# A two-block transformer kernel: token sums, head sums, gate scaling and turned blocks of the first mixer rearranged

## The reference

```python
h = rms_norm(x, g_mix_norm[l])
z = h @ w_in[l]
q_lat, kv_lat, k_rope = z[..., :o1], z[..., o1:o2], z[..., o2:o3]
uv, pin = z[..., o3:o4], z[..., o4:]
a = mla_mixer(q_lat, kv_lat, k_rope, ...)      # 4 heads: latents normed, up-projected, heads normed,
                                               # rope, causal softmax(q k / sqrt(96)) @ v -> 512 columns
gm = sgu_mixer(uv, g_v, w_spatial, b_spatial)  # below -> 256 columns
po = pool_mixer(pin, w_pool, pool_scale)       # running means over 2, 4, 8, 16 tokens, times w_pool -> 256
mix = concatenate([rms_norm(a, g_out_mla[l]), rms_norm(gm, g_out_sgu[l]), rms_norm(po, g_out_pool[l])])
x = x + mix @ w_out[l]
x = x + (silu(rms_norm(x) @ w_gate[l]) * (rms_norm(x) @ w_up[l])) @ w_down[l]

# sgu_mixer:
v = rms_norm(v, g_v)
w = w_spatial * tril(ones(128, 128))
z = einsum('hts,bcshd->bcthd', w, v_in_chunks_of_128) + b_spatial
return u * z
```

## Time and profile before

| | us |
|---|---|
| runs of the kernel | 3192.84, 3186.21, 3187.82 (median 3187.82) |
| the profiled execution, its own time | 3193.49 |
| its span in the profile | 3191.7 |
| mean granted TensorE clock | 0.986 |
| busy share of the span | PE 98%, PEld 79%, POOL 60%, DVE 47%, ACT 23% |
| chain that ended last, by engine | PE 89%, DVE 6%, issue 2%, ACT 2% |

### The profile page before, as it was taken

One profiled execution on the slowest core, in us unless ns is written; L12 is line 12 of the kernel. 1 busy time (PEld: TensorE's weight loads), 2 busy tenths in 40 slices (PEclk: granted clock), 3 DMA queues, 4 the chain that ended last, 5 costly groups with the idle time before them and its releaser, 6 DMA issues.

```text
span 3191.7 us, 41998 instructions
## 1 busy us (share of the span) xinstructions
PE 3132.2 (98%) x15408; PEld 2520.4 (79%) x15408; DVE 1498.8 (47%) x2570; ACT 739.4 (23%) x1525; POOL 1903.7 (60%) x885
## 2 busy tenths in 40 slices
PE   8999999999999999999999999999999999999998
PEld 7778888877888888876588888888787668888887
DVE  4664430356453042886545554214388653545411
ACT  4410100331010033434701101012343560111000
POOL 4277787427877877001088777787700118878775
PEclk9999999989999999999999999999999999999999
DMA  3133232103232222112032323332211103332332
GB/s 123 47 101 99 93 98 98 67 27 102 98 99 94 97 91 94 48 34 80 8 94 98 101 96 94 99 99 86 93 47 42 66 17 96 99 96 97 99 93 85
DMA packets 71716, 262.99 MB, mean 82 GB/s; under 512 B 8208, under 2 KB 8208, under 8 KB 71440
## 3 DMA queue, kind: packets, MB, share of 16 engines
q1 hardware_dynamic: 71280, 258.86, 25.2%
q10 hardware_dynamic: 288, 2.11, 0.2%
HBM read 258.85 MB, written 2.10 MB: 82 GB/s over the span
## 4 chain that ended last, share of the span: by engine, by line
PE 89%; DVE 6%; issue 2%; ACT 2%; POOL 0%; DMA 0%; SPq 0%; DVEq 0%; ACTq 0%; POOLq 0%
PE bank L639 88%; PE bank L1264 1%; DVE arena L1957 1%; DVE h_lo L1981 1%; DVE rope L1957 1%; DVE rope L1954 0%; DVE arena L2489 0%; ACT arena L1894 0%; DVE bank L1957 0%; DVE arena L2317 0%; DVE arena L2505 0%; DVE w_lo L2343 0%; PE bank L924 0%; ACT arena L1880 0%; DVE arena L1954 0%
## 5 line engine op out<-in xcount | busy, mean ns | idle before, releaser
L1401 POOL TENSOR_TENSOR w_hi<-ring,one 128x1024 fp32r<-128x1024 f32 x430 | 817.7, 1902 | 1222.3 <-PE bank L639 1167.3
L1407 POOL TENSOR_TENSOR w_lo<-ring,w_hi 128x1024 fp32r<-128x1024 f32 x422 | 1040.7, 2466 | 33.1
L639 PE MATMUL bank<-h_hi,w_hi 128*128 128x512 f32 x2256 | 895.3, 397 | 4.6 <-DVE h_lo L1981 2.5
L639 PE MATMUL bank<-h_hi,w_lo 128*128 128x512 f32 x2256 | 881.1, 391 | 0.0
L639 PE MATMUL bank<-h_lo,w_hi 128*128 128x512 f32 x2256 | 880.3, 390 | 0.0
L639 PE MATMUL bank<-act_hi,w_hi 128*128 128x512 f32 (+1 forms) x1376 | 511.6, 399 | 3.6 <-POOL w_lo L1407 3.6
L639 PEld LDWEIGHTS bank<-h_hi,w_hi 128*128 128x128 f32 x2256 | 424.0, 188 | 99.2 <-issue 5.5
L639 PEld LDWEIGHTS bank<-h_hi,w_lo 128*128 128x128 f32 x2256 | 423.7, 188 | 91.3
L639 PEld LDWEIGHTS bank<-h_lo,w_hi 128*128 128x128 f32 x2256 | 424.3, 188 | 85.1 <-issue 1.0
L639 PE MATMUL bank<-act_hi,w_lo 128*128 (+1 forms) x1120 | 440.4, 393 | 0.0
L639 PE MATMUL bank<-act_lo,w_hi 128*128 (+1 forms) x1120 | 421.0, 390 | 1.4 <-DVE act_lo L2524 1.4
(11 more groups left out here) (245 smaller groups left out, 3038.4 us busy)
## 6 DMA issues: line engine op xcount, KB each, us to landing
ring<-wstream SPq DMA_DIRECT2D x480, 512.0 KB, 3.5
par<-params SPq DMA_DIRECT2D x4, 656.5 KB, 4.8
x<-xT SPq DMA_DIRECT2D x4, 512.0 KB, 7.1
outT<-h SPq DMA_DIRECT2D x4, 512.0 KB, 2.7
cst<-const ACTq DMA_DIRECT2D x1, 1412.0 KB, 9.2
par<-params ACTq DMA_DIRECT2D x1, 652.5 KB, 5.5
arena<-pos SPq DMA_DIRECT2D x1, 256.0 KB, 2.5
cst<-const SPq DMA_DIRECT2D x1, 24.5 KB, 2.3
```

What stands on the lines that cost most here:

```text
L639: return pe.matmul(out, lhsT, rhs, start=start, stop=stop)
L1401: return po.tensor_tensor(out, a, one.broadcast_to([P, n]), ALU.mult)
L1407: po.tensor_tensor(pair_[1], raw, pair_[0].bitcast(F32), ALU.subtract).then_inc(done.sem, 1)
```

## The change

1. **Start of the mixer.** `lat_sum(0)` goes from in front of tile 3 to behind `norm_spread`; `lat_sum(1)` and the sum for the rotated key go from in front of `values(0)` to behind `lat_spread(0)`.
2. **Gate.** The gate's v is scaled by 1/rms on ScalarE (four operations) and no more on VectorE; the gain, a number for each column, is multiplied in where the bias is added, so that this addition becomes an operation with two steps.
3. **Turned blocks.** Key blocks 1 and 3 (384 and 128 columns) share a bank, so that there are three groups of transposes and copies instead of four for each pair of heads. `pv_pair` takes key blocks in the order 0, 1, 3, 2.
4. **Mix.** VectorE adds the squares (blocks 0 + 1 + 2 + 3, 4 + 5, 6 + 7) ahead of the token sums, five additions in all, so that each sum is four products. The head part of output block 0 goes ahead of the spreads and of the head sum; the other first parts follow in turn, with the third spread between the two of the rest. VectorE makes the low halves of head blocks 2 and 3 before the variance, and ScalarE makes their high halves before their squares.

```diff
-PT0 = [0, 4 * P, 7 * P, 9 * P]
+PT0 = [0, 4 * P, 8 * P, 7 * P]
+TURNS = ((0,), (1, 3), (2,))
+TURN0 = [(PT0[g[0]], sum(NT - st for st in g) * P) for g in TURNS]
...
-mx_v = signal("mix_variance", 1)
+mx_v = signal("mix_squares_added_and_variance", 6)
...
         pe.wait_ge(*n_ac(2 * l, ND - 2))
         pe.wait_ge(*n_sq(2 * l, ND))
         norm_sum(2 * l, (0, ND - 1))
-        lat_sum(0)
         dense(3, 3)
         norm_spread(2 * l)
+        lat_sum(0)
+        values(0)
+        lat_spread(0)
         lat_sum(1)
         pe.wait_ge(*z_sq(l, 4))
         token_sums(bank[5], [(m1["sqkr"], slice(0, 32))]).then_inc(kr_ss.sem, 1)
-        values(0)
-        lat_spread(0)
         values(1)
         lat_spread(1)
         pe.wait_ge(*tile_in(l, 0, PER1, 6))
...
-        def turn_pair(w, st):
-            if st == 0:
+        def turn_pair(w, g):
+            if g == 0:
...
             for e in range(2):
-                c = 8 * w + 2 * st + e
+                c = 6 * w + 2 * g + e
...
-                for t in range(st, NT):
-                    off = PS0[t] + st * P
-                    last = pe.transpose(bank[e][:, (t - st) * P:(t - st + 1) * P],
-                                        nprob[w][e][:, off:off + P], C("ident"))
+                for st in TURNS[g]:
+                    at = PT0[st] - TURN0[g][0]
+                    for t in range(st, NT):
+                        off = PS0[t] + st * P
+                        last = pe.transpose(bank[e][:, at + (t - st) * P:at + (t - st + 1) * P],
+                                            nprob[w][e][:, off:off + P], C("ident"))
...
-            for st in range(NT):
-                pe.wait_ge(*at_o(l, 8 * w + 2 * st + 2))
+            for st in (0, 1, 3, 2):
+                pe.wait_ge(*at_o(l, 6 * w + 2 * (0, 1, 2, 1)[st] + 2))
...
-                                   aprobT[e][:, PT0[st]:PT0[st] + (NT - st) * P], st == 0, st == NT - 1)
+                                   aprobT[e][:, PT0[st]:PT0[st] + (NT - st) * P], st == 0, st == 2)
...
-        MIXED = ((4, 5), (6, 7), (0, 1, 2, 3))
+        MIXED = (4, 6, 0)
...
-            pe.wait_ge(*((sg_sq, pl_q, mx_sq)[i](l, (2, 2, 4)[i])))
-            token_sums(bank[(4, 6, 5)[i]], [(mixsq[:, c, :], ALL) for c in MIXED[i]]).then_inc(mx_ss.sem, 1)
+            pe.wait_ge(*mx_v(l, (3, 3, 6)[i]))
+            token_sums(bank[(4, 6, 5)[i]], [(mixsq[:, MIXED[i], :], ALL)]).then_inc(mx_ss.sem, 1)
...
         turn_pair(0, 2)
-        turn_pair(0, 3)
...
         dense(18, 9, (4, 5))
+        dense(18, 9, (6, 7))
         turn_pair(1, 2)
-        dense(18, 9, (6, 7))
-        turn_pair(1, 3)
...
-                pe.wait_ge(*at_o(l, 16))
+                pe.wait_ge(*at_o(l, 12))
...
-        mix_spread(0)
-        mix_spread(1)
-        mix_sum(2)
...
             return last
         pe.wait_ge(*wo_r(l, 4))
+        pe.wait_ge(*mx_sq(l, 4))
         for j in range(2):
             pe.wait_ge(*w1_split(l, 10 + j + 1))
             out_part(j, 1, heads_bank(j)).then_inc(wo_a.sem, 1)
+            if j == 0:
+                mix_spread(0)
+                mix_spread(1)
+                mix_sum(2)
+        pe.wait_ge(*wo_r(l, ND))
+        out_part(0, 0, rest_bank(0)).then_inc(wo_mm.sem, 1)
         mix_spread(2)
-        pe.wait_ge(*wo_r(l, ND))
-        for j in range(2):
-            out_part(j, 0, rest_bank(j)).then_inc(wo_mm.sem, 1)
+        out_part(1, 0, rest_bank(1)).then_inc(wo_mm.sem, 1)
         for j in range(2, ND):
             pe.wait_ge(*w1_split(l, 10 + j + 1))
             if j == 2:
...
+        sc.wait_ge(*sg_rs(l, 1))
+        for m in range(NT):
+            sc.activation(m1["v"][:, m, :], m1["v"][:, m, :], ACT.Copy, scale=sg_rstd[:, m:m + 1])\
+                .then_inc(sg_v.sem, 1)
...
-        def copy_pair(w, st):
-            if w and st == 0:
+        def copy_pair(w, g):
+            at, n = TURN0[g]
+            if w and g == 0:
...
             for e in range(2):
-                sc.wait_ge(*at_t(l, 8 * w + 2 * st + e + 1))
-                sc.activation(aprobT[e][:, PT0[st]:PT0[st] + (NT - st) * P],
-                              bank[e][:, 0:(NT - st) * P], ACT.Copy).then_inc(at_o.sem, 1)
+                sc.wait_ge(*at_t(l, 6 * w + 2 * g + e + 1))
+                sc.activation(aprobT[e][:, at:at + n], bank[e][:, 0:n], ACT.Copy).then_inc(at_o.sem, 1)
...
         copy_pair(0, 1)
         exp_pair(1, 3)
         copy_pair(0, 2)
-        copy_pair(0, 3)
         for c in range(2):
             out_square(c)
             out_high(c)
-        for st in range(NT):
-            copy_pair(1, st)
+        for g in range(3):
+            copy_pair(1, g)
         copy_z(18, m1["u"][:, 1, :])
         for b in range(2):
             col = par[:, PAR1["pool_scale"]][:, b:b + 1]
...
             sc.wait_ge(*sg_g(l, b + 1))
             sc.activation(mixsq[:, 4 + b, :], mix[:, 4 + b, :], ACT.Square).then_inc(sg_sq.sem, 1)
         for c in (2, 3):
-            out_square(c)
-        sc.wait_ge(*mx_v(l, 1))
+            sc.wait_ge(*at_v(l, 2))
+            out_high(c)
+        sc.wait_ge(*mx_v(l, 4))
         sc.activation(four(mx_std, 0), four(mx_std, 0), ACT.Sqrt).then_inc(mx_sd.sem, 1)
         sc.wait_ge(*mx_ss(l, 2))
         std(four(mx_std, 1), bank[6], 1 / 256, mx_sd)
         for c in (2, 3):
-            out_high(c)
+            sc.wait_ge(*wo_r(l, c + 1))
+            out_square(c)
         for c in range(4, ND):
             sc.wait_ge(*mx_n(l, c - 3))
             sc.activation(mix_hi[c], mix[:, c, :], ACT.Copy).then_inc(wo_h.sem, 1)
...
-        ve.wait_ge(*sg_rs(l, 1))
-        for m in range(NT):
-            ve.scalar_tensor_tensor(m1["v"][:, m, :], m1["v"][:, m, :], sg_rstd[:, m:m + 1],
-                                    par[:, PAR1["g_sgu"]], ALU.mult, ALU.mult).then_inc(sg_v.sem, 1)
...
-            add(v.rearrange("p (a b) -> p a b", a=NT), bank[4 + b][:, :].rearrange("p (a b) -> p a b", a=NT),
-                bias).then_inc(sg_z.sem, 1)
+            ve.scalar_tensor_tensor(v.rearrange("p (a b) -> p a b", a=NT),
+                                    bank[4 + b][:, :].rearrange("p (a b) -> p a b", a=NT), gain("g_sgu", b),
+                                    bias, ALU.mult, ALU.add).then_inc(sg_z.sem, 1)
...
         assert steps[0] == pw.per, steps[0]
         gate_values(1)
+        def squares_joined(c, d):
+
+            add(mixsq[:, c, :], mixsq[:, c, :], mixsq[:, d, :]).then_inc(mx_v.sem, 1)
+
+        squares_joined(0, 1)
+        ve.wait_ge(*pl_q(l, 2))
+        squares_joined(6, 7)
+        ve.wait_ge(*sg_sq(l, 2))
+        squares_joined(4, 5)
+        low_part_of(2)
         ve.wait_ge(*mx_ss(l, 1))
         variance(four(mx_std, 0), bank[4][:, 0:NT], 1 / 256, mx_v)
+        low_part_of(3)
         for i in range(2):
             ve.wait_ge(*mx_sd(l, i + 1))
             inverse(mx_rc, four(mx_rstd, i), four(mx_std, i))
+        for c in (2, 3):
+            ve.wait_ge(*mx_sq(l, c + 1))
+            ve.wait_ge(*mx_v(l, c + (-1 if c == 2 else 2)))
+            squares_joined(0, c)
         ve.wait_ge(*pl_o(l, 2))
         for i in range(2):
             ve.wait_ge(*mx_rs(l, i + 1))
             for c in ((4, 5), (6, 7))[i]:
                 normed(mix[:, c, :], mix[:, c, :], gain("g_out", c), bank[(4, 6)[i]][:, :], mx_n)
-        low_part_of(2)
-        low_part_of(3)
+        for n in range(4, ND):
+            low_part_of(n)
         ve.wait_ge(*mx_sd(l, 3))
         inverse(mx_rc, four(mx_rstd, 2), four(mx_std, 2))
-        for n in range(4, ND):
-            low_part_of(n)
         def joined(j):
```

More of the change, by code:

```diff
@@ L62 @@
     ("g_in", ND), ("g_q", 2), ("g_kv", 1), ("g_qn", 1), ("g_qr", 1), ("g_kn", 1), ("g_kr", 1), ("pool_scale", 2), ("g_out", ND),
-    ("g_ffn", ND), ("g_sgu", 256), ("w_sp", 4 * P), ("b_sp", 2 * P), ("w_pool", 256)])
+    ("g_ffn", ND), ("g_sgu", 2), ("w_sp", 4 * P), ("b_sp", 2 * P), ("w_pool", 256)])
 PAR2, NPAR2 = columns([
@@ L360, in build @@
         at_c = signal("attention_pair_scaled", 2)
-        at_t = signal("attention_block_turned", 16)
-        at_o = signal("attention_block_copied", 16)
+        at_t = signal("attention_block_turned", 12)
+        at_o = signal("attention_block_copied", 12)
         at_v = signal("attention_pair_pv", 2)
@@ L2785 @@
             "g_out": np.concatenate([by_block(a[n][l]) for n in ("g_out_mla", "g_out_sgu", "g_out_pool")], 1),
-            "g_ffn": by_block(a["g_ffn_norm"][l]), "g_sgu": np.broadcast_to(a["g_sgu_v"][l], (P, 256)),
+            "g_ffn": by_block(a["g_ffn_norm"][l]), "g_sgu": by_block(a["g_sgu_v"][l]),
             "w_sp": a["w_spatial"][l].transpose(2, 0, 1).reshape(P, 4 * P),
```

## The result

The changed kernel took 3171.8 us (median of four runs, 3168.64 to 3174.44) against 3187.02 before, a ratio of 0.9946 (95% interval 0.9927 to 0.9964). In a second series it was 3174.34 against 3185.74, 0.9961 (0.9946 to 0.9976). The gain is 11 to 15 us. The profiled execution took 3174.38 with a span of 3172.6, 19.1 less than the span before; TensorE is still busy 98%.

The account below looks back on a forecast made before the run. TensorE, busy 98% of the span, was taken as the bound. Gains of 9.7 us in pass 1 and 17.6 in pass 2, together 27.3, took the profiled 3193.49 to 3166; range 3158 to 3178.

Parts of the forecast that it names:

- Start: Start of the mixer: 16 instead of 32 one-column records ahead of tile 3, gain 3.2 us in pass 1, 3.1 in pass 2.
- my own sign: Sign at the mixer's start: the prediction is wrong if the clock is at 0.5 in tile 3.
- First mask: Attention scores: with v's scalings moved to ScalarE, TensorE's 0.64 us wait for the first mask goes, gain 0.7 in each pass.
- Turned blocks: Attention transposes: three groups instead of four save a hand-over, 0.6 us for the first pair of heads, 0.2 for the second.
- Meeting of VectorE and GpSimd: End of the pool means: GpSimd's earlier split delays VectorE's tiny steps, so the pool product waits, losing 1.4 us each pass.
- the rival in which the low half also wins: Pool means: GpSimd's low half also beats VectorE's last step, the pool product waits 3.8 us, total 3172.5; chance 0.20.
- Mix: Value products' end to w_out's undisturbed run: 22.8 us against 29.21 and 30.84, gains 6.4 and 8.0, mostly the heads' sum.
- the 2.0 that I took: Mix: clock loss in us expected after the new 2.4 us wait, bounds 0 and 5.2.
- Scores of pass 2: Pass 2's scores to last transposes: with one of two waits gone, full clock expected, gain 6.35 us against the profile.
- the clock still falls in the scores, one pass: Rival: the clock falls in the scores despite one wait fewer; one pass 3172.5 us, both 3178.9; chance 0.17.

Follow-up runs that it names:

- The two runs that moved one engine or the other: Changed kernel with the gate's first values made behind the pool means, 3174.38 us; changed kernel with GpSimd's second w_out split held until squares are added, 3169.72 us.
- the last run: Changed kernel with GpSimd's split held, first two output blocks' banks exchanged and unused TensorE work in two waits: 3159.02 us, ratio 0.9906.

## Why the prediction was right, and where it was off

The time was inside the range (3158 to 3178), 5.6 us above the 3166 given; against the profile I forecast 27.3 and measured 19.1, against the medians 21 and 15.2. Most stages in which no clock fell came out as worked out; how near the whole time came is in part luck, for the unchanged part of the program alone varies by 14 us (below). That the median run before lacked the loss in pass 2's scores, as I took it, no run shows, for only one execution of that kernel was profiled.

- *Start, 3.2 and 3.1.* Measured 1.64 and 3.20 in this profile; 23 of the 24 passes with the new order take the 25.2 of pass 2. The step and its size are right, but by my own sign (clock at 0.5 in tile 3) the prediction was wrong in pass 1: 16 records can be followed by the fall as well.
- *First mask, 0.7.* Measured 0.70 and, undone, 0.71. Right in the scores; but part of the meeting hangs on this step, and takes 0.3 of it back.
- *Turned blocks, 0.6 and 0.2.* 0.63 and 0.0: the groups between parts of tile 18 cost TensorE nothing. But the step hangs together with the next one. I had worked the meeting out from these gains, but not what leaving one of them out would bring: undone, it takes the meeting with it, and each pass gains 1.0. As an edit by itself it made this kernel slower.
- *Meeting of VectorE and GpSimd, -1.4 in each pass.* Measured -1.66 and -1.64, with the order of events forecast from the earlier trace rows: the tiny step beats the low half. The two runs that moved one engine or the other removed it. I had given the rival in which the low half also wins 0.20; no pass shows it.
- *Mix, 6.4 and 8.0.* Measured 6.67 and 8.46, every wait within 0.35 us of its working, and the clock's loss about 1.5 (22.54 and 22.38 against 20.98) for the 2.0 that I took. (19.8 + 1.1 is 20.9, not 20.8, a slip without weight.) What I did not work out is which half pays. I thought of the first head part as filling the time in which 1/rms is made; it is worth 0.5 to 0.7, and that only because the clock comes back sooner, for the wait it runs into, for ScalarE's squares, is longer than the one that it covers.
- *Scores of pass 2, 6.35.* This is the step that failed. Scores and turned blocks of pass 2 gained 2.9 instead of 7.65 (0.7 + 0.6 + 6.35), because the clock fell again, behind the one wait that was left. One wait fewer is not full clock: of the 20 passes without filled waits that have only the second wait, it fell in 6, of the 4 with both waits in 1. What decides in which pass it falls stays open. The rival "the clock still falls in the scores, one pass" (0.17) happened, and I had read a chance event of one profile as a cost that the change removes. Its size is right: 4.8 to 6.4 us in the seven.
- *Not in the sum.* 1.6 us gained ahead of the scores in pass 1 (39.09 for 40.71, a fall at the head sums that appears in some passes of every kernel) and 3.6 lost behind the first block, in instructions that are the same.

The Trainium skill ("TensorE: Matmul & The Clock Gate", Part 1) says that the number of slow products varies from run to run. The trace agrees: the unchanged code behind pass 2 took between 2418.3 and 2432.5 us in these kernels' profiles, a spread as wide as the whole gain of the change.

**Where the gain lies.** Span times mean granted clock gives an estimate of the time at full clock. It counts waits at the lower clock as if they shrank too, and as the clock is listed to 0.001, one run is good to 1.6 us. Nine runs of before give 3145 to 3149, nine of the changed kernel 3143 to 3145, the five with split held and banks exchanged 3136 to 3139, the four with filled waits 3138 to 3140. So of the change's 11 to 15 us only 2 to 3 are fewer instructions and waits. The stages say the same: the mix of before at full clock would be 22.7 (29.21 less 3.2 for the heads' sum, 2.4 for the products and 0.9 for the 16 spreads, 2.84 instead of 1.95; 22.4 by the estimate used with the experiments), that of the changed kernel is 20.98 with its wait filled; 0.7 + 0.63 - 1.65 + 1.7 in each pass gives 1.4, so 2.8 in all. The rest is clock: 3.2 in most passes at the start, and in the mix about 5 in pass 1 (6.67 less 1.7), where the lower clock lasted 13.7 us before and 3.4 after. Of the heads' sum, 32 one-column records in 6.83 us that became 8 in 0.95, 3.2 are clock and the rest fewer records. These clock gains add up to more than the 11 to 15; the unchanged stages took part of them back (3.6 in this profile).

## What to carry to other kernels

Count one-column sums by what they do to the clock of the products behind them, and add squares elementwise first where another engine is idle: 40 records fewer (24 for 64) took 6 to 8 us out of each mix. A gain on the bounding engine moves the moment at which it frees buffers, and so when other engines start; look what that start will now collide with, for here 0.64 us gained cost 1.65, and holding back a split that nobody waits for yet gave most of it back. A reorder that gains can do so by the clock alone: compare it at equal clock before it is called a better order. One profile's fall of the clock is a draw: before it is booked as removable, look at the same stage in the other passes and runs.

## What was not expected of the hardware

With useless products in two waits the mean granted clock was 0.993 to 0.997 instead of 0.990 to 0.993, and the median 9.5 us of 3168 shorter, some 6 of which are accounted for. The clock fell in the mix even where no wait stood beside 16 one-column records (the last run, pass 2). A 16-column step of VectorE beside a GpSimd operation took 1.75 us, and 0.17 without; between two GpSimd operations in a row VectorE got one such step in (128.59, ahead of 128.60), as in the earlier trace rows.
